# The end of the attention layers ordered by token tile, and the dense stage begun on the first tile

## What is computed

```
for l in range(2):
    h = rms_norm(x, g_mix[l])
    A, B, C, D = four attention groups of 4 heads from h @ w_in[l]   # 256 features each
    groups = [rms_norm(o, g_out[l, i]) for i, o in enumerate((A, B, C, D))]
    x = x + concatenate(groups) @ w_out[l]                           # 1024 x 1024
    h2 = rms_norm(x, g_ffn[l])
    if l == 0:  x = x + (silu(h2 @ w_gate) * (h2 @ w_up)) @ w_down   # 2816 hidden columns
    else:       x = x + top-2-of-8 experts of the same form          # 3584 hidden columns each
```

## Time and profile before

| | |
|---|---|
| Median of 3 runs | 1596.38 us (1595.97 to 1606.27) |
| Profiled execution | 1602.95 us, span 1601.2 us |
| PE busy | 1525.2 us, 95% of the span |
| DVE, ACT busy | 1105.7 us (69%), 910.6 us (57%) |
| Mean granted clock of PE | 0.98 |
| DMA | 424.75 MB, mean 265 GB/s |

### The profile page before, as it was taken

The page is one execution under the profiler, slowest core; times in us unless marked ns, Lnnn a source line. Parts: engine busy times, 40 slices in busy tenths (PEclk is TensorE's granted clock), DMA queues, the critical chain, the costliest instruction groups (busy, mean ns, idle before and its releaser), DMA issues.

```text
span 1601.2 us, 17106 instructions
## 1 busy us (share of the span) xinstructions
PE 1525.2 (95%) x6723; PEld 1176.4 (73%) x6723; DVE 1105.7 (69%) x1260; ACT 910.6 (57%) x1213; POOL 42.2 (3%) x77
## 2 busy tenths in 40 slices
PE   6899799998999779999999999999999999999997
PEld 3565588885565468887887887887887887788785
DVE  1244364442333369888888989988888889888894
ACT  2133353341233267776776776776776777767672
POOL 1020000000021000000000000000000000000000
PEclk9899999999999889999999999999999999999999
DMA  7710474419040249999999999999999999999982
GB/s 234 277 53 0 158 263 158 158 61 398 1 150 8 105 177 383 334 366 337 341 368 333 354 342 342 373 335 341 359 329 359 355 334 365 339 334 369 333 305 81
DMA packets 178907, 424.75 MB, mean 265 GB/s; under 512 B 6224, under 2 KB 11528, under 8 KB 178696
## 3 DMA queue, kind: packets, MB, share of 16 engines
q1 hardware_dynamic: 178824, 423.63, 72.7%
HBM read 422.57 MB, written 1.06 MB: 265 GB/s over the span
## 4 chain that ended last, share of the span: by engine, by line
PE 90%; DVE 4%; DMA 2%; ACT 2%; issue 1%; SPq 1%; POOL 0%; DVEq 0%; POOLq 0%; ACTq 0%
PE ps L899 13%; PE ps L901 13%; PE ps L900 13%; PE ps L826 8%; PE ps L828 8%; PE ps L827 8%; PE ps L611 7%; PE ps L734 3%; PE ps L803 3%; PE ps L804 3%; PE ps L802 3%; DMA wmem<-in_w_in_dram 2%; PE ps L877 2%; PE ps L811 2%; PE ps L912 2%
## 5 line engine op out<-in xcount | busy, mean ns | idle before, releaser
L1492 DVE TENSOR_TENSOR unit_rounded<-wmem,unit_rounded 128x1024 fp32r<-128x1024 f32 (+1 forms) x744 | 854.2, 1210 | 109.1 <-ACT unit_rounded L1102 108.9
L1102 ACT ACTIVATE unit_rounded<-wmem 128x1024 fp32r<-128x1024 f32 (+1 forms) x744 | 719.7, 1042 | 141.8 <-PE ps L901 73.7
L826 PE MATMUL ps<-unit_rounded,vbuf_rounded 128*128 128x512 f32 x536 | 212.5, 396 | 4.5 <-DVE unit_rounded L1492 3.0
L827 PE MATMUL ps<-unit_rounded,vbuf_rounded 128*128 128x512 f32 x536 | 212.6, 397 | 0.0
L828 PE MATMUL ps<-unit_rounded,stage_rounded 128*128 128x512 f32 x536 | 212.6, 397 | 0.0
L899 PE MATMUL ps<-unit_rounded,qkT_rounded 128*128 128x512 f32 x448 | 180.6, 403 | 0.0
L899 PE MATMUL ps<-unit_rounded,hT_rounded 128*128 128x512 f32 x448 | 178.7, 399 | 0.0
L901 PE MATMUL ps<-unit_rounded,qkT_rounded 128*128 128x512 f32 x448 | 177.0, 395 | 0.0
L900 PE MATMUL ps<-unit_rounded,qkT_rounded 128*128 128x512 f32 x448 | 177.0, 395 | 0.0
L901 PE MATMUL ps<-unit_rounded,hT_rounded 128*128 128x512 f32 x448 | 174.7, 390 | 0.0
L900 PE MATMUL ps<-unit_rounded,hT_rounded 128*128 128x512 f32 x448 | 174.5, 389 | 0.0
(11 more groups left out here) (184 smaller groups left out, 1394.0 us busy)
## 6 DMA issues: line engine op xcount, KB each, us to landing
wmem<-in_w_exp_gate_dram SPq DMA_DIRECT2D x56, 2048.0 KB, 7.9
wmem<-in_w_exp_up_dram SPq DMA_DIRECT2D x56, 2048.0 KB, 8.5
wmem<-in_w_exp_down_dram SPq DMA_DIRECT2D x56, 2048.0 KB, 8.3
wmem<-in_w_in_dram SPq DMA_DIRECT2D x4, 3072.0 KB, 16.2
wmem<-in_w_ff_gate_dram SPq DMA_DIRECT2D x5, 2048.0 KB, 8.1
wmem<-in_w_ff_up_dram SPq DMA_DIRECT2D x5, 2048.0 KB, 9.0
wmem<-in_w_ff_down_dram SPq DMA_DIRECT2D x5, 2048.0 KB, 7.6
wmem<-in_w_out_dram SPq DMA_DIRECT2D x4, 2048.0 KB, 19.2
```

Of the source, the lines that this page charges most:

```text
L826: pe.matmul(o, hhb, hi[:, b, c], start=(first and b == 0), stop=False, skip_group_check=True)
L827: pe.matmul(o, hhb, lo[:, b, c], start=False, stop=False, skip_group_check=True)
L1102: act.activation(quarter_r(HIGH[l][kind], q, cols), quarter(SETS[l][i][kind], q, cols), ACT.Copy).then_inc(hi_ready[kind], 1)
L1492: dve.tensor_tensor(quarter_r(u, q, cols), quarter(u, q, cols), quarter_r(HIGH[l][kind], q, cols), ALU.subtract).then_inc(lo_ready[kind], 1)
```

## The change

1. **Output projection by tile.** On PE, tile 1's groups A and C move. Before B's probability transposes stands only D of tile 1, then A after B's values, then B of tile 0, then C of tile 1, the norm transposes of tile 0 (fills 0 and 1), and last B of tile 1. PE then waits until fills 0 and 1 are read; it waited for 2 and 3.
2. **Norm by tile.** ACT and DVE read tile 0's fills before they square, add and scale tile 1. PE's fills 2 and 3 are a function of their own, `second_norm`, with `second_ready` as the wait for their reading. In layer 1 both follow the attention at once.
3. **Dense stage.** The first step's order on PE is: gate of tile 0, fills 2 and 3, up of tile 0, the wait for their reading, gate of tile 1, transposes of tile 0, up of tile 1, down of tile 0, transposes of tile 1. The first step has 512 columns and the second one 256. So the weights split in the tail are of full size (two kinds on ACT, `first_high`); on DVE gate's low part stays ahead of `read_p(l, "B")`, up's low part comes after `group_out(l, 3, "B")`. The loads of the first step are of full size, those of the second half.
4. **Written out.** The six dense steps are written out on every engine and on SP's queue; the loops are gone there.

The diff, with blank context lines and the guards of `unless_last` (which now also knows that there is no loop) left out:

```diff
-            peeled = n - 4
+            peeled = n if n == DENSE_STEPS else n - 4
             for s in range(peeled):
                 one(s, (parity + s) % 2, first + s, use + (parity + s) // 2, None)
+            if peeled == n:
+                return
...
         def hidden_cols(s, dense):
-            return FT // 2 if dense and s == 0 else FT
+            return FT // 2 if dense and s == 1 else FT
...
-            def first_steps(l, gate, up, down, cols):
+            def first_steps(l, gate, up, down, second):
+                cols = FT
...
                 sp.wait_ge(sc_full, l * NSU + SUSE["out"] + 1)
-                load_up(gate, l, 1, 0, cols)
-                load_up(up, l, 1, 1, cols)
+                load_up(gate, l, 1, 0, cols, second)
+                load_up(up, l, 1, 1, cols, second)
                 if l == 0:
-                    load_down(down, l, 1, cols)
+                    load_down(down, l, 1, cols, second)
...
-            with sp.Fori(1, DENSE_STEPS // 2) as i:
-                f0 = i * (2 * FT) - FT // 2
-                step(0, 0, (0, 1, 2), dense, f0, sp.snap(i * 2))
-                step(0, 1, (0, 1, 2), dense, f0 + FT, sp.snap(i * 2 + 1))
+            for s in range(2, DENSE_STEPS):
+                step(0, s % 2, (0, 1, 2), dense, s * FT - FT // 2, s)
...
-            def norm(l, name):
-                for i in range(4):
+            def norm(l, name, parts=range(4)):
+                for i in parts:
...
                 out_project(l, 0, ["C"])
-                out_project(l, 1, ["D", "A"])
+                out_project(l, 1, ["D"])
                 p_transposes(l, "B")
                 values(l, 3, "B")
-                out_project(l, 1, ["C"])
+                out_project(l, 1, ["A"])
                 o_transposes(l, 3, "B")
                 out_project(l, 0, ["B"])
+                out_project(l, 1, ["C"])
+                norm(l, "y", (0, 1))
                 out_project(l, 1, ["B"])
-                norm(l, "y")
+                emptied(pe, l, ("y", 0))
+                emptied(pe, l, ("y", 1))
+
+            def second_norm(l):
+                norm(l, "y", (2, 3))
+
+            def second_ready(l):
                 emptied(pe, l, ("y", 2))
                 emptied(pe, l, ("y", 3))
...
                 def one(s, i, step, use_, _):
                     cols = hidden_cols(s, l == 0)
+                    if l == 0 and s == 0:
+                        gate_up(l, i, step, 0, src, 0, cols, 1, (0,))
+                        second_norm(l)
+                        gate_up(l, i, step, 0, src, 0, cols, 1, (1,))
+                        second_ready(l)
+                        gate_up(l, i, step, 1, src, 1, cols, 1, (0,))
+                        transposes(0, cols, step * 2 + 1, 1)
+                        gate_up(l, i, step, 1, src, 1, cols, 1, (1,))
+                        down(l, i, step, 0, 0, cols, step * 2 + 1, 1, first=True)
+                        transposes(1, cols, step * 2 + 2, 1)
+                        return
...
             attention(1)
+            second_norm(1)
+            second_ready(1)
...
                     act.activation(squares[y][t], x[:, t, :], ACT.Square, accum_out=ssx[:, t:t + 1]).then_inc(ssx_ready, 1)
-                act.wait_ge(gains, 1)
...
+                    if y:
+                        for i in (2 * t, 2 * t + 1) if parts else (2 * t + 1,):
+                            read(i)
+                if not y:
+                    act.wait_ge(gains, 1)
+                    for t in range(NT):
+                        read(2 * t + 1)
...
                 softmax(l, 3, "B")
-                for kind in range(2 - l):
-                    low(l, 0, kind, l * DENSE_STEPS, hidden_cols(0, l == 0))
+                low(l, 0, 0, l * DENSE_STEPS)
                 read_p(l, "B")
                 inverse(l, "B")
                 group_out(l, 3, "B")
+                if l == 0:
+                    low(0, 0, 1, 0)
                 for t in range(NT):
                     add_out(l, t)
                     norm_scale(l, "y", t)
-                norm_read(l, "y")
+                    norm_read(l, "y", (t,))
```

More of the change, by code:

```diff
@@ L381, in unless_last @@
         def unless_last(eng, s, n, loop, run):
+            if loop is None:
+                if s < n - 1:
+                    run()
+                return
             if s < n - 3:
@@ L779, in attention, with gate_up @@
                 out_project(l, 0, ["C"])
-                out_project(l, 1, ["D", "A"])
+                out_project(l, 1, ["D"])
                 p_transposes(l, "B")
                 values(l, 3, "B")
-                out_project(l, 1, ["C"])
+                out_project(l, 1, ["A"])
                 o_transposes(l, 3, "B")
                 out_project(l, 0, ["B"])
+                out_project(l, 1, ["C"])
+                norm(l, "y", (0, 1))
                 out_project(l, 1, ["B"])
-                norm(l, "y")
+                emptied(pe, l, ("y", 0))
[3 more added lines that the diff above has]
+            def second_ready(l):
                 emptied(pe, l, ("y", 2))
                 emptied(pe, l, ("y", 3))
-            def gate_up(l, i, step, bufs, src, t, cols, count):
-                for kind, full in ((0, g_full), (1, u_full)):
+            def gate_up(l, i, step, bufs, src, t, cols, count, kinds=(0, 1)):
+                for kind in kinds:
+                    full = (g_full, u_full)[kind]
                     hi, lo = weight(HIGH[l][kind], kind, cols), weight(SETS[l][i][kind], kind, cols)
@@ L961, in norm, with read @@
                 y = name == "y"
+                parts = y and l == 0
+                def read(i):
+                    t = i // 2
+                    filled(act, l, (name, i))
+                    for b in range(4):
+                        k = 4 * (i % 2) + b
+                        c = (G_FFN if y else G_MIX) + l * KD + k
+                        ins = act.activation((xh_r if parts else hT)[:, k, t * P:(t + 1) * P],
+                                             bank((name, i))[:, b * P:(b + 1) * P], ACT.Copy, scale=gT[:, c:c + 1])
+                    ins.then_inc(xh_ready if parts else tr_free[1], 1)
                 for t in range(NT):
@@ L1126, in one @@
                     hidden_high(0, step * 2 + 1, 1, cols)
-                    unless_last(act, s, n, loop, lambda: high(l, 1 - i, 0, step + 1, use_ + i))
+                    after = hidden_cols(s + 1, l == 0)
+                    unless_last(act, s, n, loop, lambda: high(l, 1 - i, 0, step + 1, use_ + i, after))
                     silu(1, step * 2 + 2, 1, cols)
-                    unless_last(act, s, n, loop, lambda: high(l, 1 - i, 1, step + 1, use_ + i))
+                    unless_last(act, s, n, loop, lambda: high(l, 1 - i, 1, step + 1, use_ + i, after))
                     hidden_high(1, step * 2 + 2, 1, cols)
@@ L1256, in norm_scale, with norm_read @@
                 dve.tensor_scalar(xs[:, t, :], x[:, t, :], rx[:, t:t + 1], None, ALU.mult).then_inc(xs_ready, 1)
-            def norm_read(l, name):
+            def norm_read(l, name, ts=range(NT)):
                 c0 = (G_FFN if name == "y" else G_MIX) + l * KD
                 if name == "y" and l == 0:
-                    for i in range(4):
+                    for i in [2 * t + half for t in ts for half in range(2)]:
                         t = i // 2
@@ L1273, in norm_read @@
                     return
-                for i in (0, 2):
+                for i in [2 * t for t in ts]:
                     t = i // 2
@@ L1511, in one @@
                     hidden_low(0, step * 2 + 1, 1, cols)
-                    unless_last(dve, s, n, loop, lambda: low(l, 1 - i, 0, step + 1))
+                    after = hidden_cols(s + 1, l == 0)
+                    unless_last(dve, s, n, loop, lambda: low(l, 1 - i, 0, step + 1, after))
                     hidden(1, step * 2 + 2, 1, cols)
-                    unless_last(dve, s, n, loop, lambda: low(l, 1 - i, 1, step + 1))
+                    unless_last(dve, s, n, loop, lambda: low(l, 1 - i, 1, step + 1, after))
                     hidden_low(1, step * 2 + 2, 1, cols)
```

11 lines of the change are left out of this document (1 added, 10 removed).

## The result

| | before | changed |
|---|---|---|
| Median (12 runs each) | 1597.92 us (1594.48 to 1607.71) | 1588.92 us (1586.88 to 1593.55) |
| Ratio, 95% interval | | 0.993 [0.9912, 0.9949] |
| Profiled execution, span | 1602.95 us, 1601.2 us | 1591.42 us, 1589.5 us |
| Mean granted clock of that execution | 0.980 | 0.985 |

The changed kernel is 9.0 us faster by the medians, 8 to 14 us by the interval; 7.0 was forecast. The time lies in the stated range, the change is larger than the sum gave. That the median itself came within 0.5 us of the 1589.4 forecast is partly luck: the forecast started from a median of three runs of before, 1596.38, which lies 1.5 us under that of twelve, and this offset hid most of the 2.0 us by which the gain was put too low.

What follows compares the result with a forecast made beforehand. The kernel was taken as bound by PE's instruction stream, with time to win only at its standstills or lower clock. Layer 0's -8.9 and layer 1's +1.9 gave -7.0 us: 1589.4 from median 1596.38, range 1585 to 1597.5.

Steps and rivals of the forecast that it cites:

- Part 1 (earlier group B): Both layers' tails: DVE reads group B's first transposed head 2.3 us earlier; moved low parts and larger loads cost 0.
- Part 2 (dense start): Layer 0's tail: with the norm by tile, the dense stage starts at 181.2 instead of 188.53, 7.3 us earlier.
- Cover for tile 1's norm: Layer 0: tile 1's norm is ready at 185.5, PE asks for it at 186.8, leaving 1.3 us.
- Part 3 (step order): First dense steps: 3.2 us of first-step loss vanish, a 0.5 us stall comes in step 1; layer 0 in sum -8.9.
- Rival (b): Dense stage: step order gives nothing, the 3.2 us lost return in the half-size second step; 1592.1 us, chance 0.12.
- Unrolling: Dense stage: writing out all six steps changes the time by 0, bounds -0.5 and +1 us.
- Part 4 (layer 1): Layer 1's tail: the router needs both tiles, so the tile order makes it 1.9 us later, 4.2 without part 1.
- rival (a): Group B's light stretch: the clock halves ahead of the projections, costing 3.35 us per layer; 1592.8 or 1596.1 us, chance 0.22.
- The mis-sized term is the clock: Layer 0's first dense step: 2.8 us of its work at half clock before, so 1.4 us lost that would vanish.
- The profile's start: Untouched stretches keep the profiled execution's times; as a sign, layer 1's router starts 7.0 us earlier than 551.38.
- The measurement: Whole kernel: a measurement tells about 1% (16 us) from no change; chances 0.03 faster, 0.94 same, 0.03 slower.
- Rival (c): After B's light stretch the clock stays down over projections and first dense gate, losing 10.2 us; 1599.6 us, chance 0.06.

Runs made afterwards that it cites:

- before_filled: The kernel before with dummy 512-column matmuls in PE's waits in both layers' tails, order unchanged; median 1597.4 us, ratio to before 0.9959.
- half_first: The changed kernel with the half-size dense step first again, its loads, high and low parts of half size too; median 1590.9 us, ratio to before 0.996.
- unrolled_only: The kernel before with only the six dense steps written out; median 1598.9 us, ratio to before 0.9989.
- second profile: Profile of the changed kernel run once more, unchanged; median of those runs 1590.9 us, ratio to before 0.9936.
- set B: Second group of runs, on one chip beside its own 24 runs of before (median 1601.2 us); the unchanged changed kernel had median 1590.9 us there.
- after_filled: The changed kernel with four dummy matmuls in layer 1 between tile 1's projection and its norm transposes; median 1594.0 us, ratio to before 0.9943.
- combined: The changed kernel with layer 1's old tail order, DVE's first fill read during tile 1's squares, dummy matmuls in five places; median 1585.6 us, ratio to before 0.9888.
- combined_again: The combined kernel repeated unchanged as a control on another chip; median 1582.8 us, ratio to before 0.9882.
- after_again: The changed kernel run once more, unchanged, as a control; median 1590.9 us, ratio to before 0.9936.

## Why the prediction was right, and where its size was off

- **Part 1 (earlier group B).** -2.3 forecast, 2.36 measured in both layers. Up's low behind the group output was hidden, the doubled high parts too (7.67 us from 132.51 on ACT, 3.46 us of idle left).
- **Part 2 (dense start).** 7.3 us earlier forecast, 2.36+5.58 = 7.9 measured. The 0.6 is from adding busy lengths with modelled ends: 1.09+3.56 was in starts 0.93+3.20 (172.97, 173.90, 177.10). Cover for tile 1's norm 1.3 forecast, 1.15 measured.
- **Part 3 (step order).** 0.5 us of stall forecast in step 1, 0.6 measured; layer 0 in sum -8.9 and -9.1. The dense stage itself was to be 1.6 us shorter and is 1.18. before_filled, with the old order at 1.00 throughout, took 186.50, so 1.28 of before's 187.78 were the clock. The changed kernel took 186.60 with 1.04 of norm transposes in it, so the step order gives 0.94: together 2.2 of the 2.7 us of loss that were to go. Rival (b) would have made it 188.9; 186.60 speaks against it, and half_first's 188.99 shows what the place of the half step is worth.
- **Unrolling.** 0 forecast. unrolled_only's interval holds it without excluding a gain of some us; its dense stage less the clock is equal to before's within 0.1 us.
- **Part 4 (layer 1).** +1.9 forecast, +2.6 measured (3.5 in the second profile). The difference is half clock, which the forecast didn't have: 0.85 us in the second tile's transposes in the first profile, 1.5 us by rival (a) in the second. Without it the order costs 1.8.
- **The mis-sized term is the clock.** The sum gave it 1.4 us, from the one drop of the profiled execution at 184.5. The mean half-clock time is 54 to 57 us in before's runs and 45 in the changed kernel's: 9 to 12 us, at 0.5 each 4.6 to 5.8 us. Order alone (touched stretches without the clock in them: -9.1+1.4 and +2.6-0.85) is -5.9, the sum 10.5 to 11.7; the means differ by 10.8 (first runs) and 9.7 to 10.2 (set B, without and with the run at 0.931). I took one profile for the typical one, and its drops at 112.9 and 478 for fixed.
- **The profile's start.** The forecast took all of the profiled execution's untouched stretches as fixed. They differ by 5.2 us between the two profiles, 1.4 of it the wait for group A's weights, and the router came 11.7 us earlier where 7.0 was named as the sign.
- **The measurement** was put at telling 1% from no change. The interval came out at 0.0037 wide, so a gain of 0.7% is clear of noise.
- **Rival (a)** happens: in layer 0 in 3 of the 10 profiles with the early group B (after_filled, combined, combined_again: 14.72, 14.73, 13.11 us against 9.98), in layer 1 in 1 of 5 (after_again: 11.52), and in none of the stretches without it (4 in layer 0, 9 in layer 1). Its price was put at 3.35 us; it was 3.1 to 4.7 in layer 0 and 1.5 in layer 1. It is no rival to the gain but a part of the changed kernel's spread. The Trainium skill's sentence that a transpose doesn't count as busy for the clock in the same way (TensorE: Matmul & The Clock Gate, PE-mode transpose) fits these four; the eleven others, with the same transposes, kept 1.00 there, so the transposes alone don't decide it.
- **Rival (c)** was not seen. Direct proof that a given run's extra time is a drop is only there for profiled runs; for the others it rests on their mean granted clock.

## What to carry to other kernels

A reordering that frees a piece of work and one that opens a wait belong together: here each alone gave nothing or a loss, and both gave 9 to 11 us, because the freed group filled the wait. Apply such an order only where the next stage can start on the first part: in layer 1 the router can't, and the old order there is 1.8 us better, 2.6 to 3.5 with the clock. And read how much of a span is at half clock in several executions before taking a hole for its idle time alone: a hole in PE's stream costs its length and, in a part of the runs, the clock behind it, and dummy matmuls in the waits recovered 4 to 6 us of it here (0.988 against 0.9915, with overlapping intervals). Look in the same profiles for a load whose arrival varies, before a difference between two of them is put down to the change or to the clock.

## What was not expected of the hardware

- The same kernel differs from run to run by up to 14 us, and where and how long PE is at half clock goes with it (after_again 1584.7 to 1598.6, mean clock 0.989 to 0.983). The Trainium skill (TensorE: Matmul & The Clock Gate, What's actually happening) calls the slow phase at a kernel's start run-variable and puts its penalty below 1% of a typical span. The drops here are others, behind light stretches in mid-kernel: before's mean half-clock time was 54 to 57 us of 1600, at 0.5 up to 1.8%; about 20 us of it is the router's own light stretch.
- The load of group A's weights in layer 0 arrived with a spread of 9 us between profiles of equal order (wait of 5.2 to 14.6 us), as much as the whole change gives.
- Dummy matmuls of 512 columns in waits held the clock at 1.00 through a tail that fell to 0.50 without them, with 0.69 us of PE's wait left over; ahead of the router's light work they only moved the drop.
